# New step marks and TensorE shares for the expert-gather stream that runs beside a decoder layer

## What is computed

```python
n = rmsnorm(x)                       # D = 1024
proj = n @ w_in                      # attention q/k/v, GLA q/k/v, gates
oa = sliding window attention        # window 128, 16 heads, 4 kv heads
og = gated linear attention          # 4 heads, state 128 x 256 each
h = x + (sigmoid(ga) * oa + sigmoid(gb) * rmsnorm(og) * silu(rb)) @ w_out
q = rmsnorm(h) @ peer_wq             # 8 heads, two halves of 128
# top 16 of 128 keys per half, top 16 of the sums: 128 experts per token
y = h + sum over 128 experts of  g * gelu(u[e] . n2) * v[e]
```

## Time and profile before

| | |
|---|---|
| median of 3 runs | 3679.12 us (3675.5 to 3683.36) |
| the profiled execution | 3668.51 us, of which the span from first to last instruction is 3666.6 us |
| busy in the span | PE 2825.5 us, DVE 2725.1 us, POOL 2062.2 us, ACT 738.5 us |
| gathers and loads | 1297.17 MB, mean 354 GB/s |

### The profile page before, as it was taken

One profiled execution on the slowest core, in us unless ns is written; L12 is line 12 of the kernel. 1 busy time (PEld: TensorE's weight loads), 2 busy tenths in 40 slices (PEclk: granted clock), 3 DMA queues, 4 the chain that ended last, 5 costly groups with the idle time before them and its releaser, 6 DMA issues.

```text
span 3666.6 us, 33338 instructions
## 1 busy us (share of the span) xinstructions
PE 2825.5 (77%) x9988; PEld 1790.9 (49%) x9988; DVE 2725.1 (74%) x5917; ACT 738.5 (20%) x1783; POOL 2062.2 (56%) x1820
## 2 busy tenths in 40 slices
PE   7888679888796998788998687868878645555555
PEld 6777556556663665443665254535566311111111
DVE  0631777897888856886889898779778867777777
ACT  1321112423211223222211111323211111101011
POOL 0000067777666656655666677667676656555553
PEclk9899889999898988888999788989889877777777
DMA  4124399999999989889999999999999898999998
GB/s 149 47 81 166 110 382 412 384 377 399 421 420 396 395 351 373 322 311 364 420 402 410 338 402 420 391 348 375 404 421 420 337 379 345 427 427 427 427 427 341
DMA packets 305121, 1297.17 MB, mean 354 GB/s; under 512 B 35384, under 2 KB 44624, under 8 KB 252048
## 3 DMA queue, kind: packets, MB, share of 16 engines
q0 software_dynamic: 260352, 1082.25, 74.2%
q1 hardware_dynamic: 44592, 212.81, 15.0%
HBM read 1279.33 MB, written 17.66 MB: 354 GB/s over the span
## 4 chain that ended last, share of the span: by engine, by line
PE 29%; DVE 27%; DMA 18%; issue 12%; another core or an unknown queue 6%; DVEq 3%; POOL 3%; ACT 2%; ACTq 0%; SPq 0%; PEldq 0%; PEld 0%; POOLq 0%
DVE ringb L1568 8%; DMA ringb<-in_uv,eidx 8%; PE vsum L959 8%; PE bank L1049 7%; DVE acc L1614 6%; PE bank L1089 4%; DMA wring<-in_uv,eidx 2%; POOL ringb L778 2%; PE bank L1246 2%; PE n2p L1049 1%; DVE scT L2001 1%; DMA ringb<-in_v,eidx 1%; DMA qkb<-in_uv,eidx 1%; DMA arena<-in_uv,eidx 1%
## 5 line engine op out<-in xcount | busy, mean ns | idle before, releaser
L959 PE MATMUL vsum<-ringb,diag 128*128 128x512 f32 x1672 | 914.9, 690 | 324.0 <-ACT diag L1293 200.7
L778 POOL DMA_INDIRECT ringb<-in_u,eidx x627 | 677.0, 1080 | 767.3 <-DVE eidx L1693 453.2
L778 POOL DMA_INDIRECT ringb<-in_v,eidx x654 | 715.5, 1094 | 375.1 <-issue 179.6
L1568 DVE SCALAR_TENSOR_TENSOR ringb<-ringb,n2p 128x1024 f32<-128x1024 f32 x627 | 741.1, 1216 | 55.5 <-issue 20.8
L959 PEld LDWEIGHTS vsum<-ringb,diag 128*128 128x128 f32 x1672 | 341.8, 216 | 800.3 <-issue 457.5
L1049 PE MATMUL bank<-wring,nTb 128*128 128x256 f32 (+1 forms) x2768 | 633.2, 389 | 34.7 <-DMA wring<-in_w 25.6
L1049 PEld LDWEIGHTS bank<-wring,nTb 128*128 128x128 f32 (+1 forms) x2768 | 501.1, 183 | 169.2 <-issue 34.1
L1614 DVE SCALAR_TENSOR_TENSOR acc<-ringb,wgt,acc 128x1024 f32<-128x1024 f32 x314 | 402.7, 1283 | 12.3 <-issue 6.2
L1293 ACT ACTIVATE diag<-cst,wgt 128x128 f32<-128x128 f32 x535 | 203.5, 397 | 878.9 <-DVE wgt L1584 622.5
L761 POOL DMA_INDIRECT ringb<-in_uv,eidx x156 | 228.4, 1464 | 183.4 <-DVE vgb L1614 92.7
L1089 PE MATMUL bank<-nTb,wring 128*128 128x256 f32 (+1 forms) x1056 | 246.2, 389 | 29.9 <-issue 24.9
(11 more groups left out here) (393 smaller groups left out, 3767.3 us busy)
## 6 DMA issues: line engine op xcount, KB each, us to landing
wring<-in_w SPq DMA_DIRECT2D x152, 1024.0 KB
ringb<-in_v,eidx POOLq DMA_INDIRECT x654
ringb<-in_u,eidx POOLq DMA_INDIRECT x627
n2t<-scratch_n SPq DMA_DIRECT2D x14, 512.0 KB
oab<-in_xp SPq DMA_DIRECT2D x4, 1024.0 KB, 5.9
bTb<-in_keysT SPq DMA_DIRECT2D x4, 1024.0 KB
vgb<-in_xp SPq DMA_DIRECT2D x4, 1024.0 KB, 8.9
arena<-in_s SPq DMA_DIRECT2D x8, 512.0 KB, 6.1
```

What stands on the lines that cost most here:

```text
L778: pool.indirect_dma_start(out=ring[r], out_offset=None, in_=a["u"] if kind == "u" else a["v"], in_offset=place)\
L959: last = mm(out[:, g * 512:(g + 1) * 512], lhs, row[:, g * 512:(g + 1) * 512], start=(x == first), stop=(x == end))
L1568: STT(row, row, 1.0, n2, ALU.mult, ALU.mult, accum_out=dg[:, m % 2, at:at + 1]).then_inc(used(("u", x))[0], 1)
```

## The change

Two tables replace two rules. First, the weights of the stages' points come from `LENGTH`, a number of steps per stage and part, which is divided evenly over the stage's points; part 1's `gla` gets 34.3. Second, `BY_PE` has a table for each part. The sums of a `LENGTH` table are the steps of the part, so that the entry of a stage is about the steps that it gets.

```diff
+LENGTH = {1: {"norm": 1.0, "fm": 13.3, "va": 1.3, "at": 20.6, "gate": 4.2, "gla": 34.3, "rb": 4.8, "gb": 5.3, "mg": 1.1, "wo": 4.5, "n2": 0.5, "q": 21.5, "rt": 7.7},
+          2: {"norm": 1.1, "fm": 12.0, "va": 2.0, "at": 16.7, "gate": 3.7, "gla": 30.9, "sgla": 3.9, "rb": 7.6, "gb": 8.1, "mg": 1.3, "wo": 7.4, "n2": 1.0, "q": 16.6, "sr": 9.2, "rt": 6.5},
+          3: {"norm": 1.1, "fm": 24.1, "va": 1.4, "at": 22.4, "gate": 4.4, "gla": 36.7, "rb": 4.9, "gb": 5.4, "mg": 1.1, "wo": 4.7, "n2": 0.5, "q": 23.2, "rt": 8.1}}
+
+def stage_keys(c):
...
 def stages(c):
-    s = c == SC
-    tokens = lambda w: w + 6 * s
-    out = [(("norm", i), 12) for i in range(2)]
-    out += [(("fm", b), 13 if c == SC + 1 else 10) for b in range(FMB)] + [(("va", 0), tokens(10))]
-    out += [(("at", n, i), (tokens(10) if i == 0 and n % CH[c] == 0 else 10) + 3 * s) for n in range(4 * CH[c] + 2) for i in range(2)]
-    out += [(("gate", i), 13) for i in range(3)]
-    out += [(("gla", n, i), tokens(10) if i == 4 and ga_after(c, n) is not None else 10) for n in range(len(gla_units(c))) for i in range(6)]
...
-    return out
+    keys = stage_keys(c)
+    return [(k, LENGTH[max(1, c)].get(k[0], 1) / sum(x[0] == k[0] for x in keys)) for k in keys]
...
-        out[k] = lo + (hi - lo) * done // total
+        out[k] = lo + int((hi - lo) * done / total)
...
-BY_PE = {"norm": 2.0, "fm": 0.8, "va": 0.8, "at": 1.0, "gate": 2.0, "gla": 1.45, "sgla": 1.3, "rb": 0.0, "gb": 0.0, "mg": 0.0,
-         "wo": 0.0, "n2": 0.5, "q": 1.2, "sr": 2.0, "rt": 2.0}
+BY_PE = {1: {"norm": 2.0, "fm": 0.09, "va": 0.0, "at": 0.65, "gate": 1.97, "gla": 1.44, "rb": 0.0, "gb": 0.0, "mg": 1.23, "wo": 0.0, "n2": 2.0, "q": 1.03, "rt": 2.0},
+         2: {"norm": 2.0, "fm": 0.0, "va": 0.0, "at": 0.0, "gate": 1.97, "gla": 1.28, "sgla": 0.71, "rb": 0.0, "gb": 0.0, "mg": 1.2, "wo": 0.0, "n2": 1.93, "q": 0.73, "sr": 2.0, "rt": 2.0},
+         3: {"norm": 2.0, "fm": 0.98, "va": 0.0, "at": 0.72, "gate": 1.94, "gla": 1.44, "rb": 0.0, "gb": 0.0, "mg": 1.25, "wo": 0.0, "n2": 2.0, "q": 1.06, "rt": 2.0}}
...
-                    rate[q] = BY_PE[last[0]]
+                    rate[q] = BY_PE[c][last[0]]
```

More of the change, by code:

```diff
@@ L204, in together @@
     return ("between", 0) == mixer_order(c)[-1]
-def stages(c):
-    s = c == SC
-    tokens = lambda w: w + 6 * s
-    out = [(("norm", i), 12) for i in range(2)]
-    out += [(("fm", b), 13 if c == SC + 1 else 10) for b in range(FMB)] + [(("va", 0), tokens(10))]
-    out += [(("at", n, i), (tokens(10) if i == 0 and n % CH[c] == 0 else 10) + 3 * s) for n in range(4 * CH[c] + 2) for i in range(2)]
-    out += [(("gate", i), 13) for i in range(3)]
-    out += [(("gla", n, i), tokens(10) if i == 4 and ga_after(c, n) is not None else 10) for n in range(len(gla_units(c))) for i in range(6)]
[L216 to L220, removed]
-    return out
+LENGTH = {1: {"norm": 1.0, "fm": 13.3, "va": 1.3, "at": 20.6, "gate": 4.2, "gla": 34.3, "rb": 4.8, "gb": 5.3, "mg": 1.1, "wo": 4.5, "n2": 0.5, "q": 21.5, "rt": 7.7},
+          2: {"norm": 1.1, "fm": 12.0, "va": 2.0, "at": 16.7, "gate": 3.7, "gla": 30.9, "sgla": 3.9, "rb": 7.6, "gb": 8.1, "mg": 1.3, "wo": 7.4, "n2": 1.0, "q": 16.6, "sr": 9.2, "rt": 6.5},
+          3: {"norm": 1.1, "fm": 24.1, "va": 1.4, "at": 22.4, "gate": 4.4, "gla": 36.7, "rb": 4.9, "gb": 5.4, "mg": 1.1, "wo": 4.7, "n2": 0.5, "q": 23.2, "rt": 8.1}}
+def stage_keys(c):
+    s = c == SC
+    out = [("norm", i) for i in range(2)] + [("fm", b) for b in range(FMB)] + [("va", 0)]
+    out += [("at", n, i) for n in range(4 * CH[c] + 2) for i in range(2)] + [("gate", i) for i in range(3)]
+    out += [("gla", n, i) for n in range(len(gla_units(c))) for i in range(6)] + ([("sgla", b) for b in range(NS + 1)] if s else [])
+    out += [("rb", u) for u in range(4)] + [("gb", u) for u in range(4)] + [("mg", 0)]
+    out += [("wo", u) for u in range(4)] + [("n2", i) for i in range(2)]
+    return out + [("q", q) for q in range(HC + 1)] + ([("sr", g) for g in range(4)] if s else []) + [("rt", i) for i in range(12)]
+def stages(c):
+    keys = stage_keys(c)
+    return [(k, LENGTH[max(1, c)].get(k[0], 1) / sum(x[0] == k[0] for x in keys)) for k in keys]
 def marks(c):
```

## The result

The changed kernel took 3745.09 us (median of 4, 3729.79 to 3757.49), the kernel before 3679.65 beside it: ratio 1.0176, 95% interval 1.0139 to 1.0213. It is slower by 65 us where I forecast 73 us less, and 55 us above the upper end of the range. The profiled execution took 76.6 us more by its span.

A forecast was written before the change was run, and what follows sets the result against it. Memory traffic, at most 427 GB/s, was taken as the bound wherever engines allow. Parts of -5, -36 and -32 us summed to -73, from 3668.5 profiled to 3595, plus 10.6 for the median: 3606 us, range 3550 to 3690.

The forecast's parts named there:

- G: Gate and recurrence stages of each part: forecast +37, +16 and +32 us, together +85 for 31 added steps.
- my point of decision: Price per step added to G, 158/31 = 5.1 us, separating the forecast gain from the rival of a slower kernel.
- Traffic is the bound wherever the engines let it be: Whole kernel: no single engine bounds it; memory traffic does, with a ceiling of 427 GB/s.
- POOL's price: Gathers: 0.94 + 0.30 = 1.24 us each on POOL, plus 0.5 us per v row on DVE in G.
- DVE and PE fill their waits of now: In G: added steps fit both engines' gaps, so 31 steps cost +85 us, 2.7 us each.
- at, part 2, -45: Part 2's attention: 23 to 16 steps and no row on PE, lasting 125 us, 45 less.
- sgla, -20: Part 2's chain through loads of states: 10 to 4 steps, 9 us idle kept, 56 us, 20 less.
- A, -55: First group of each part, routing included: fewer steps, forecast -23, -12 and -20 us.
- B, -12: Group of stages after G, taken as traffic-bound: forecast -10, +18 and -20 us in the three parts.
- Q, -20: Last group of each part: steps -2, +2 and -3, forecast -10, +7 and -17 us.
- The port, a rival: Each of 51 rows moved to DVE holds POOL 0.7 us, losing 36 us of gain: 3642; chance 0.13.
- The steps in G cost what they cost now: Rival: G's 31 steps cost 205 us at 6.2, 7.3, 6.4 each, the rest returns 158: 3726; chance 0.18.

The follow-up runs named there:

- e18: Changed kernel with three chained GpSimd memsets of 128 x 96 ahead of each of the recurrences' 408 gathers; ratio 1.0668 to the kernel before.
- e19: Kernel before with the same three chained GpSimd memsets of 128 x 96 ahead of each of the recurrences' 288 gathers; ratio 1.0333.
- e1: Changed kernel with its new marks but the old TensorE shares of rows; ratio 1.0174 to the kernel before.
- e12: Changed kernel with TensorE taking all v rows of the recurrences (share 2.0); ratio 1.0116 to the kernel before.
- e6: Changed kernel with two more places in TensorE's recurrence program to run its steps, so in smaller pieces; ratio 1.0174 to the kernel before.
- e7: Changed kernel with ScalarE computing the next unit's decays ahead of its last steps in the recurrence; ratio 1.0222 to the kernel before.
- e10: Changed kernel with a drain and a 96-column memset on GpSimd ahead of each of the recurrences' 408 gathers; ratio 1.4451 to the kernel before.
- e14: Changed kernel with six already-met semaphore waits on GpSimd ahead of each of the recurrences' 408 gathers; ratio 1.0171 to the kernel before.
- e16: Changed kernel with one 32 x 1 memset on GpSimd, no drain, ahead of the first 384 gathers of the recurrences' steps; ratio 1.0165.
- e15: Kernel before with six already-met semaphore waits on GpSimd ahead of each of the recurrences' 288 gathers; ratio 1.0000.
- e8: Kernel before, unchanged, run for a trace on the chip of e6 and e7; 3689.81 us.

## Why the prediction was wrong

The span came out 77 us longer for a forecast 73 shorter, a miss of 150. Of it 57 us lie in G, and 91 in the other groups: B 33, at 27, A 13, Q 10, sgla 8. Two steps failed. In G the sums left no idle time, and on this chip 54 us of it stayed. Outside G they credited the steps taken away at nearly their full price, 158/31 = 5.1 us each, and 67/31 = 2.2 came out (2.0 on the later chip). A step added to G cost 142/31 = 4.6 us (4.1 on the later chip), below my point of decision of 5.1; it loses because a step elsewhere gives back less than half of that.

- *Traffic is the bound wherever the engines let it be*: right in B of parts 1 and 3 and in the tail, 420 and 427 GB/s before and after. In the recurrences POOL's issue is the limit: e18 and e19 show it on a chip of the faster kind, where POOL is occupied nearly all of G.
- *POOL's price*: I took 1.24 us and a supplement for L1614 alone; L1991 and L1995 hold the port too. The row that I had gives (132.39 + 118 x 0.3) / 118 = 1.42 us a gather, and the runs without filler show 1.36 to 1.47 in every recurrence with DVE rows as here. The sum bore it all the same: by the trace 109 gathers more start in G (107 in the sums) and take POOL 149 us more (146), so this is not what failed.
- *DVE and PE fill their waits of now*: they did, their busy times are as summed. But G was priced by POOL's time alone, with its idle time put at nothing: 554 us before, of which 491 were POOL's, and 639 after. On the first chip POOL was free for 61 us of G before and for 54 of 692 after. In part 1's recurrence those are mostly waits for TensorE to free buffers and for releases not named. So the term that failed is this idle time, 54 us for 0. On the later chip POOL was free for 29 us before and 8 after, and G came out at 651 us. That this is near 639 is in part luck: the kernel before needed only 525 there, so that +126 and not +85 led to it.
- *at, part 2, -45*: -29.5 and -8.9. It takes 145 to 147 us with 16 steps whatever the shares are: 145.4 in e1 with PE busy 138 us at clock 0.85, 146.5 in the changed kernel with PE busy 124 at 0.70. The prediction had this as a thing that would make it wrong. PE's 103 us were mis-sized too: its own work took longer at a granted clock of 0.70 (0.69 on the later chip), so at the level of 1.2 GHz for much of the time, after its rows had been taken away. In e1, with PE busy 138 of 145 us, PE itself may be the bound; which chain holds the others was not tried.
- *sgla, -20*: -11.5 and -7.3, the same thing: it takes 74 to 79 us with 4 steps for 86 with 10. On the first chip PE was busy 57 us in it for the 47 of the sum, at a clock of 0.79 for 0.87, and 17 us stayed idle for the 9 kept.
- *A, -55*: -42 and -65, right in size.
- *B, -12*: +21 and +11. Parts 1 and 3 run at 421 GB/s as said, but gave back less than their steps: on the later chip POOL issued 6 and 11 gathers fewer where the steps need 8 and 16 fewer. What the ring is short of after G is made up in B; I had credited it to G and not charged it to B. e19 shows it enlarged: B of part 1 takes 152 us for 136, with 97 gathers for 84. Part 2's B came out at +29 and +25 for +18, at 398 GB/s; why it is not full there stays open.
- *Q, -20*: -10 and +3. Part 2's came out at +16 and +15 for the +7, DVE being busy 187 us in it.
- *The port, a rival*: real (e12), but its price was in every gather of before already. The shares cost nothing beside the new marks (e1) and 16 us beside the old ones (e2).
- *The steps in G cost what they cost now*: the nearest rival, 3726 for 3745, but near by luck: it had +205 in G and -158 elsewhere, and +142 and -67 came out. Its prices were 6.2, 7.3, 6.4 us a step; 6.2, 3.2 and 4.4 came out. Its reason, waits that move from one engine to the other, is not what e6 and e7 found; but on the first chip POOL's free time in G did stay.

What stays open: why at and sgla have the floors they have, why POOL is left waiting in G on the first chip and hardly on the later, and why the chips differ.

## What to carry to other kernels

Price both ends of a move: here a step cost 4.6 us where it was put and gave back 2.2 where it was taken. When the gathers' issuing engine shows no waits in a stage, its occupied time per gather is the price of each gather put there, stalls included; take that quotient from the row and not the shortest instruction. Before moving work out of a stage, ask what floor it has without that work: two stages here stayed at 145 and at 74 to 79 us, whatever the shares. And a buffer ring only defers: what one stage draws from it, the next pays.

## What the runs showed of the hardware

- In the changed kernel's trace a gather beside whose first 0.9 us DVE does nothing but dots with n2 in PSUM takes 0.94 us, at most 0.95 (222 gathers); beside L1620 alone, with both row operands in SBUF, 1.66 us on average and up to 1.99 (163 gathers).
- A drain on GpSimd behind an indirect gather waits 3.2 to 3.7 us in nine of ten cases (e10, 408 gathers), though the gather's own instruction shows 0.94 in e10's timeline: something that the drain waits for goes on after the instruction's end.
- Between two gathers 0.30 us of idle stand, and a memset of 0.12 us, or six waits already met, fit into it: the pace stays at 1.24 to 1.25 us (e14, e16).
- The kernel before took 3555 to 3558 us in five of the seven sets of runs and 3680 and 3694 in the other two, some 3.7% apart, with a mean granted clock of 0.881 (e15) against 0.866 and 0.863 (e8); the ratios of changed to before agree to 0.1% (1.0176; 1.0171 and 1.0165 with the doses of e14 and e16, which took no time).
